# Attention's triangular masks: added by TensorE in the scores' accumulation, instead of by VectorE

## The reference, cut to what matters

```
valid_w = (dpos >= 0) & (dpos < WINDOW) & (win_pos >= 0)[None, :]        # WINDOW = 512
p_w = masked_softmax(einsum('btghd,blgd->btghl', qg, k_win), valid_w)
p_s = masked_softmax(einsum('btghd,btgnd->btghn', qg, ks), kpos <= q_pos)  # TOP_K = 16 blocks: all
```

## Time and profile before

| | |
|---|---|
| median of 3 runs | 2304.37 us (2300.16 to 2312.11) |
| profiled execution, its own time | 2311.03 us |
| span of its trace | 2309.2 us |
| PE busy | 2144.4 us (93%) |
| DVE busy | 759.6 us (33%) |
| ACT busy | 475.2 us (21%) |
| POOL busy | 391.9 us (17%) |
| attention's units, in the trace | from 539.3 to 917.2 us |

### The profile page before, as it was taken

One profiled execution on the slowest core, in us unless ns is written; L12 is line 12 of the kernel. 1 busy time (PEld: TensorE's weight loads), 2 busy tenths in 40 slices (PEclk: granted clock), 3 DMA queues, 4 the chain that ended last, 5 costly groups with the idle time before them and its releaser, 6 DMA issues.

```text
span 2309.2 us, 28326 instructions
## 1 busy us (share of the span) xinstructions
PE 2144.4 (93%) x11241; PEld 1645.3 (71%) x11241; DVE 759.6 (33%) x1454; ACT 475.2 (21%) x887; POOL 391.9 (17%) x392
## 2 busy tenths in 40 slices
PE   5999999987887888999999998989999999899998
PEld 2555677765555555666676666789999999878886
DVE  3111132285656656421201125521111111134343
ACT  4000010213433434101200114421111111123232
POOL 0000021011222322221000015300000000045553
PEclk9999999995978879999989999999999999999999
DMA  9133100003100000554223434321211111135452
GB/s 354 65 129 102 53 19 19 19 1 125 29 1 1 1 1 30 154 139 124 80 81 97 115 95 155 129 55 37 54 36 54 36 54 36 42 140 170 141 174 101
DMA packets 179110, 187.67 MB, mean 81 GB/s; under 512 B 9941, under 2 KB 149309, under 8 KB 178558
## 3 DMA queue, kind: packets, MB, share of 16 engines
q1 hardware_dynamic: 177950, 182.03, 25.4%
q10 hardware_dynamic: 1056, 4.23, 0.5%
HBM read 173.88 MB, written 16.53 MB: 82 GB/s over the span
## 4 chain that ended last, share of the span: by engine, by line
PE 85%; DVE 7%; DMA 3%; issue 2%; POOL 2%; ACT 1%; SPq 1%; DVEq 0%; ACTq 0%; PEldq 0%; POOLq 0%
PE ps L2261 22%; PE ps L2181 15%; PE ps L1853 8%; PE ps L1872 6%; PE ps L2227 5%; PE ps L2228 5%; PE ps L2229 5%; PE ps L2048 3%; PE ps L2070 3%; PE ps L2031 3%; POOL arena L830 2%; DMA arena<-in_w_ada 1%; DMA arena<-in_w_out 1%; DVE arena L496 1%; PE ps L1808 1%
## 5 line engine op out<-in xcount | busy, mean ns | idle before, releaser
L2261 PE MATMUL ps<-h_hi,wup_hi 128*128 128x344 f32 x1056 | 341.6, 323 | 18.9 <-PE ps L2261 11.6
L2261 PE MATMUL ps<-h_lo,wup_hi 128*128 128x344 f32 x1056 | 340.2, 322 | 0.0
L2261 PE MATMUL ps<-h_hi,wup_lo 128*128 128x344 f32 x1056 | 339.7, 322 | 0.0
L2227 PE MATMUL ps<-rw_hi,ra_hi 128*128 128x512 f32 x540 | 217.1, 402 | 19.3 <-DVE rw_lo L1615 12.5
L2261 PEld LDWEIGHTS ps<-h_hi,wup_hi 128*128 128x128 f32 x1056 | 200.2, 190 | 25.2 <-issue 24.7
L2228 PE MATMUL ps<-rw_hi,ra_lo 128*128 128x512 f32 x540 | 215.0, 398 | 0.0
L2229 PE MATMUL ps<-rw_lo,ra_hi 128*128 128x512 f32 x540 | 214.9, 398 | 0.0
L2181 PE MATMUL ps<-hT,arena 128*128 128x344 f32 x704 | 212.0, 460 | 0.0
L862 POOL CAST ra_hi<-arena 128x384 fp32r<-128x384 f32 (+1 forms) x90 | 51.8, 576 | 941.2 <-DVE arena L1753 505.2
L2261 PEld LDWEIGHTS ps<-h_lo,wup_hi 128*128 128x128 f32 x1056 | 200.1, 190 | 0.0
L2261 PEld LDWEIGHTS ps<-h_hi,wup_lo 128*128 128x128 f32 x1056 | 199.7, 189 | 0.0
(11 more groups left out here) (386 smaller groups left out, 2543.2 us busy)
## 6 DMA issues: line engine op xcount, KB each, us to landing
hT<-in_w_down SPq DMA_DIRECT2D x66, 512.0 KB, 3.5
arena<-in_w_ada SPq DMA_DIRECT2D x12, 2048.0 KB, 8.5
arena<-in_w_up SPq DMA_DIRECT2D x44, 512.0 KB, 4.9
arena<-in_w_in SPq DMA_DIRECT2D x30, 512.0 KB, 5.3
arena<-in_w_out SPq DMA_DIRECT2D x24, 512.0 KB, 3.7
arena<-in_cache_cmp_kv SPq DMA_DIRECT2D x64, 128.0 KB, 2.1
arena<-in_cache_slc_kv SPq DMA_DIRECT2D x128, 64.0 KB, 1.9
arena<-in_w_in SPq DMA_DIRECT2D x4, 1544.0 KB, 12.4
```

Source lines behind the costliest of these rows:

```text
L2227: nc.tensor.matmul(out, ra_hi[rnd][a][:, rows], rw_hi[rnd][w][:, cols], start=(k == 0), stop=False)
L2261: ins = nc.tensor.matmul(ps[:, bank, 0:TG], w[:, k0 + k, :], h[:, k, toks], start=(k == 0 and j == 0), stop=(k == KD - 1 and j == 2))
```

## The change

The two additions on DVE and the wait behind them go. `att_S` now cuts each half of the scores where a mask begins or ends, so that a piece is either wholly masked or not at all. The pieces without a mask come first, then the masked ones, whose accumulation stays open; it is closed by a product of the identity with the mask, over all 128 rows. DVE's maximum now waits for that last product.

```diff
@@ att_max, DVE
-                ins = nc.vector.tensor_tensor(sp_[:, z - P:z], sp_[:, z - P:z], cst("causal_ts"), ALU.add)
-                if kind == 0 and i >= WIN // P:
-                    ins = nc.vector.tensor_tensor(sp_[:, a:a + P], sp_[:, a:a + P], cst("window_ts"), ALU.add)
-                step(ins)
                 if u >= 4:
                     dve.wait_ge(s_exp, t - 3)
                 nc.vector.tensor_reduce(nmx[:, u % 4:u % 4 + 1], sp_[:, a:z], AX.X, ALU.max, negate=True).then_inc(s_max, 1)
@@ att_S, PE
                 w = nb * P // 2
+
+                masks = {"causal_ts": 512 + w - P}
+                if kind == 0 and i >= WIN // P:
+                    masks["window_ts"] = 512 - w
+                pieces = []
                 for x in range(2):
-                    rows, first = slice(x * HD, (x + 1) * HD), lo * P + x * w
-                    cols = slice(512 - w, 512) if x == 0 else slice(0, w)
-                    ins = nc.tensor.matmul(ps[:, bank + x, cols], qT_[e][rows, i * P:(i + 1) * P],
-                                           kdup[1 - kind][g][rows, first:first + w], start=True, stop=True)
+                    a, z = 512 - w if x == 0 else 512, 512 if x == 0 else 512 + w
+                    cuts = sorted({a, z} | {min(max(m + y, a), z) for m in masks.values() for y in (0, P)})
+                    pieces += [(any(m <= c < m + P for m in masks.values()), x, c, d) for c, d in zip(cuts, cuts[1:])]
+                for masked, x, c, d in sorted(pieces):
+                    rows, first = slice(x * HD, (x + 1) * HD), lo * P + c - (512 - w)
+                    nc.tensor.matmul(ps[:, bank + x, c - 512 * x:d - 512 * x], qT_[e][rows, i * P:(i + 1) * P],
+                                     kdup[1 - kind][g][rows, first:first + d - c], start=True, stop=not masked)
+                for name, m in masks.items():
+                    for x in range(2):
+                        c, d = max(m, 512 - w if x == 0 else 512), min(m + P, 512 if x == 0 else 512 + w)
+                        if c < d:
+                            ins = nc.tensor.matmul(ps[:, bank + x, c - 512 * x:d - 512 * x], ident, cst(name)[:, c - m:d - m],
+                                                   start=False, stop=True)
                 ins.then_inc(s_S, 1)
```

## The result

The changed kernel takes 2334.4 us (median of 4 runs, 2331.08 to 2336.87) against 2304.0 before (4 runs): a ratio of 1.0126, 95% interval 1.0096 to 1.0157. It is slower by 30 us, where 25 were forecast; the forecast was 2329 us, and 2334.4 lies inside its range of 2308 to 2343. The profiled executions differ by 2336.9 - 2311.0 = 25.9 us.

The account below looks back on a forecast made before the run. The attention was taken as bound by a cycle through POOL, PE and DVE, by PE alone in narrow units at half clock. Additions +35.0, masks -6.0, clock -4.1 make +24.9 on 2304.4: 2329 us, range 2308 to 2343.

Parts of the forecast that it names:

- The chain: Attention stage: the path that ended last passes 69 groups of scores, 35 at full clock, and only 18 causal masks.
- The cover of the other groups: The other 59 score groups lie beside POOL's scaling and DVE's copy, so PE's additions there cost nothing.
- The price at full clock: Behind a score group at full clock: 0.375 us for one identity product, 0.585 for two, including 0.165 for changing shape.
- Additions: PE's identity products behind the 69 score groups on the critical path of the attention stage, together +35.0 us.
- the price of the narrow blocks at half clock: One identity product at half clock costs 0.62 us, or 0.42 with transposes right behind; 34 groups, 18.9 us.
- the cuts at nothing: Cutting scores into 128 more pieces costs nothing, as weights load during the pass before; at worst 7 us.
- The masks' removal: Taking DVE's masks out of the attention gains only at 18 places on the critical path, 0.335 us each: -6.0 us.
- The help of the clock: Denser PE work lets block 3 of the first and third pairs gain full clock, 2 x 2.07: -4.1 us.
- The first, that the clock pays all of it back: Blocks 1 to 3 run at full clock in all pairs: +5.1 us, 2309 us, no measurable change; chance 0.15.
- The second, DVE's list: DVE's in-order work decides in blocks 4 to 7; removing masks gives 28 us, so 2276 us; chance 0.07.
- The third, failing cover: Hidden score groups reach the critical path and cuts cost 7 us: +25 to +45, up to 2350 us; chance 0.15.

Follow-up runs that it names:

- product-first kernel: The changed kernel with the identity's product ahead of the scores, which accumulate on it; 2310.8 us, ratio 1.0022 to the kernel before.
- the run with both masks: The changed kernel with VectorE's masks put back, so that VectorE and TensorE both add them; 2358.0 us, ratio 1.0232 to the kernel before.
- idle work: Extra TensorE products at changes of pair: on the kernel before 2299.3 us, on the changed kernel 2348.4; product ahead in narrow blocks 2297.9, plus stage start 2292.6.

## Why the prediction was right, point by point

**The chain.** That PE's scores stand in the cycle and the masks don't is shown by the wide parts: without masks 133.1 against 132.7, with both masks the same 147.0 as with TensorE's alone. The cover of the other groups (PE work that costs nothing since it lies beside POOL's scaling and the copy) held there too, as the lengthening per two cycles (12.08 - 11.01 = 1.07 us for block 5, from inverse to inverse) is that of one group with one product and one with two, 0.42 + 0.64 = 1.06.

**The price at full clock** was a little low: 0.375 and 0.585 forecast, 0.42 and 0.64 on the chain. The passes were right (0.22 for a product), and the turn was 0.20, not 0.165. The Trainium skill ("TensorE: Matmul & The Clock Gate", step by step of a matmul) says that the next weights load while the current matmul runs, if row groups don't conflict or the background buffer is the target. The trace agrees where the shape stays: in the product-first kernel the load starts 0.11 us ahead of its product. At the turn it started with the product, and the 0.2 us per cycle that the product-first kernel saves are what that costs; which of the page's two conditions failed there, no run shows.

**The three sizes that were off** are the other terms. They cancelled, so that the sum came out within 6 us is luck.

(1) Additions, forecast 35.0, measured 51.7 by the run with both masks. Of its profiled 43.7, 15 lie from block 4 on, nearly as forecast (14 groups at 0.585 and 21 at 0.375, less those of narrow blocks). The step that failed is the price of the narrow blocks at half clock: 34 groups for 18.9 us with the cuts at nothing, where the narrow parts grew by 176.0 - 147.4 = 28.6. Blocks 1 and 2, which ran at half clock in the kernel before and in the one with both masks, show how. Block 2 grew by 3.16 us per pair (10.06 to 13.22). Its four groups are all on the chain, but a product cost 0.53 with transposes behind it and 0.72 without, not 0.42 and 0.62, and the cuts 0.21 in three of the four. Block 1 grew by about 2.2 per pair (8.01 to 10.23 in pair 0), 0.55 for each of its four groups, while the chain of the kernel before has only 8 of these 16 groups. The prediction says that at half clock everything PE is given is paid in full, and then prices the chain's groups alone. So groups counted as hidden came onto the chain. Blocks 0 and 3 bear the other 7 us, in which the clock has its part.

(2) The masks' removal, forecast 6.0 by the chain's 18 places, measured 13.5 alone and 21 to 24 beside TensorE's additions. Counting places on the chain missed that the narrow parts run at a higher clock without the masks.

(3) The help of the clock, forecast 4.1: it is not a term of its own but lies inside the other two.

**The rivals.** The first, that the clock pays all of it back, came true in half: pairs 1 and 2 ran their narrow parts in 34 and 32 us, 2 and 6 less than before, and pairs 0 and 3 paid 7 and 10 more. The Trainium skill (same page, on the clock gate) says that activity releases the throttle. The trace agrees for the changes of pair, which ran at 0.96 with idle work and at 0.76 without. It does not for the narrow parts, where PE had no gap in 30.7 us and stayed at half clock; in pair 3 of the changed kernel:

```profile
853.00:883.70 30.70, 30.70 (x151) 21.49 (x151) 9.87 (x27) 8.91 (x29) 6.07 (x10) 0.50 0.00 1
```

The second, DVE's list, is ruled out by the run without masks, whose wide parts gained nothing. The third, failing cover, holds in the narrow blocks: there hidden groups came onto the chain and the cuts of block 2 were paid.

What stays open is what tips a narrow part to full or half clock. The same instructions ran at 0.60 in one pair and 1.00 in another of the same execution, and idle work ahead of them didn't help: in the profiled executions of four kernels with it no narrow part behind it ran at a clearly higher clock than in the same kernel without it, and five of twelve ran lower. One profiled execution of each kernel is too little to call that an effect of the idle work.

## What to carry to other kernels

Ask first whether TensorE's instructions stand in the cycle and those of the other engine don't. In the wide blocks it was so, and moving the masks to TensorE cost 14 us with the clock at full. Then ask at which place in TensorE's list the work stands: behind a product of another array shape it costs a turn of 0.2 us over its passes, beside one of the same shape only the passes. Here the idea paid in the narrow blocks alone, product first (2293.8 against 2307), where it came with a higher clock. Where TensorE's clock is at half and it has no gap, price every instruction and not those of the chain alone, cuts too; and expect a small change on its waits to move more time than its own length (13.5 us for 6.0 here).

## What was not expected of the hardware

- A stretch can keep half clock with TensorE busy without a gap (30.70 of 30.70 us at 0.50), and block 2's list takes 8.1 us at full clock in place of 13.2, which is 0.61 of it. In the clock's levels there is nothing between.
- The product of the identity needs longer for its weights than a transpose through the identity: 213 ns on average against 151, though both are 128x128 float32. The means mix both clocks; at full clock single loads take 0.14 us in a transpose and 0.19 in the product, as the 0.30 of two that start 0.11 apart shows.

```profile
L2058 PEld LDWEIGHTS ps<-const,arena 128*128 128x128 f32 x528 | 62.4, 151 | 38.7 <-POOL arena L830 26.6 <-issue 11.0
L2041 PEld LDWEIGHTS ps<-const 128*128 128x128 f32 x352 | 55.7, 213 | 17.1 <-issue 4.6
```

- The kernel before scatters from 2296 to 2314 us over 58 runs on three chips, and its mean clock goes with it (2298.4 us at 0.957, 2313.6 at 0.948). That the scatter is the narrow parts' clock fits the traces above, but only one of these runs has a trace.
